# Turned keys stored in the order in which they are loaded, with w_out's counts, the x tiles and the sample softmax reordered

## The reference, cut to what matters

```python
z = rmsnorm(x) @ w_in                      # columns: q (4 heads x 2 x 64), k, v (4 x 128), u_a, v_a
# differential attention, per head
s = einsum(q, k) / 8 + rel_bias            # two maps m = 0, 1
a = softmax(s[0]) - lam * softmax(s[1])
o_b = rmsnorm(a @ v) * (1 - lam_init)
o_a = u_a * (tril(w_spatial) @ layernorm(v_a) + b_spatial)
x = x + rmsnorm(concat(o_b, o_a) @ w_out)
h = causal_conv3(rmsnorm(x) @ w_up); x = x + rmsnorm((silu(h_g) * h_u) @ w_down)
```

## Time and profile before

| | us |
|---|---|
| median of three timed runs | 1334.69 |
| the profiled execution, its own time | 1343.45 |
| its span from first to last instruction | 1341.7 |
| PE busy / DVE / ACT / POOL | 1314.5 / 726.9 / 447.0 / 167.2 |

### The profile page before, as it was taken

How to read it: one execution, slowest core, us unless ns; L and a number is a source line. 1 busy time by engine, 2 the same in 40 slices (tenths; PEclk the granted TensorE clock), 3 DMA queues, 4 the chain that set the end, 5 groups by cost and what they waited for, 6 DMA issues and landing times.

```text
span 1341.7 us, 21889 instructions
## 1 busy us (share of the span) xinstructions
PE 1314.5 (98%) x8364; PEld 1191.9 (89%) x8364; DVE 726.9 (54%) x1185; ACT 447.0 (33%) x764; POOL 167.2 (12%) x323
## 2 busy tenths in 40 slices
PE   7999999999997999999999999999999999999997
PEld 7999999966665888998989899998989898989986
DVE  6446645277776464466454535545464635453556
ACT  6321001057766343441323223231313131323332
POOL 2227000022222211200000000000000000000003
PEclk9999999999998999999999999999999999999999
DMA  8576778369997242321110201020201111020117
GB/s 274 180 253 239 264 221 214 75 170 252 248 261 220 78 141 71 110 79 32 40 54 16 78 16 63 16 78 16 78 16 63 31 63 31 17 77 16 47 48 137
DMA packets 132424, 146.96 MB, mean 110 GB/s; under 512 B 25852, under 2 KB 101285, under 8 KB 132357
## 3 DMA queue, kind: packets, MB, share of 16 engines
q1 hardware_dynamic: 107865, 122.30, 31.3%
q10 hardware_dynamic: 23500, 20.24, 4.7%
q0 software_dynamic: 992, 3.54, 1.6%
HBM read 114.06 MB, written 31.47 MB: 108 GB/s over the span
## 4 chain that ended last, share of the span: by engine, by line
PE 88%; SPq 4%; DMA 4%; issue 2%; DVE 1%; ACT 1%; POOL 0%; POOLq 0%; DVEq 0%; ACTq 0%
PE PS L2515 39%; PE PS L2234 17%; PE PS L2580 16%; PE PS L2459 7%; PE PS L2595 2%; PE PS L2610 2%; SPq L883 2%; DMA x_in<-in_x_prompt_dram 1%; DMA wo_raw<-in_w_out_dram 1%; DMA kt_a<-keys_t 1%; SPq L893 1%; PE PS L2285 1%; SPq L894 1%; PE PS L2325 1%; PE PS L2388 1%
## 5 line engine op out<-in xcount | busy, mean ns | idle before, releaser
L2515 PE MATMUL PS<-act_lo,wu_hi 128*128 128x364 f32 (+1 forms) x1056 | 346.4, 328 | 0.0
L2515 PE MATMUL PS<-act_hi,wu_lo 128*128 128x364 f32 (+1 forms) x1056 | 346.0, 328 | 0.0
L2515 PE MATMUL PS<-act_hi,wu_hi 128*128 128x364 f32 (+1 forms) x1056 | 345.9, 328 | 0.0
L2515 PEld LDWEIGHTS PS<-act_hi,wu_hi 128*128 128x128 f32 x1056 | 198.5, 188 | 0.5
L2515 PEld LDWEIGHTS PS<-act_lo,wu_hi 128*128 128x128 f32 x1056 | 198.2, 188 | 0.4
L2515 PEld LDWEIGHTS PS<-act_hi,wu_lo 128*128 128x128 f32 x1056 | 198.3, 188 | 0.0
L1999 DVE TENSOR_TENSOR y_acc<-y_acc,PS 128x512 f32<-128x512 f32 x162 | 111.2, 687 | 116.0 <-PE PS L2580 116.0
L2580 PE MATMUL PS<-wd_hi,g_hi 128*128 128x512 f32 x324 | 130.1, 401 | 0.0
L2580 PE MATMUL PS<-wd_lo,g_hi 128*128 128x512 f32 x324 | 128.0, 395 | 0.0
L2580 PE MATMUL PS<-wd_hi,g_lo 128*128 128x512 f32 x288 | 114.0, 396 | 0.0
L1362 ACT CAST g_hi<-conv 128x1088 fp32r<-128x1088 f32 x21 | 23.2, 1103 | 245.6 <-PE PS L2580 189.7
(11 more groups left out here) (294 smaller groups left out, 2306.4 us busy)
## 6 DMA issues: line engine op xcount, KB each, us to landing
wu_raw<-in_w_up_dram SPq DMA_DIRECT2D x44, 512.0 KB, 3.8
k_tok<-in_cache_k_dram SPq DMA_DIRECT2D x64, 256.0 KB, 3.7
keys_t<-k_turned ACTq DMA_DIRECT2D x32, 512.0 KB, 4.1
vpage<-in_cache_v_dram SPq DMA_DIRECT2D x64, 256.0 KB, 6.6
wd_raw<-in_w_down_dram SPq DMA_DIRECT2D x22, 512.0 KB, 5.3
w_raw<-in_w_in_dram SPq DMA_DIRECT2D x20, 512.0 KB, 6.4
kt_mid<-keys_t SPq DMA_DIRECT2D x20, 256.0 KB, 8.4
kt_b<-keys_t SPq DMA_DIRECT2D x20, 256.0 KB, 9.6
```

Of the source, the lines that this page charges most:

```text
L2515: mm = nc.tensor.matmul(PS[:, 3 * half + c, 0:kept(c)], a[:, half, k, :], b[:, k, KEPT[c]], start=(j == 0), stop=(j == len(parts) - 1))
```

## The change

1. `keys_t` is laid out by unit, block j, feature d, pair, part i and column c, and no longer by pair, i, d, j, c. A unit's load is then one DMA over 128 partitions in runs of 8 KB in place of four; a pair's store is four DMAs, one for each j, in place of one. The counts of `ktok_stored` and `kt_loaded` follow.
2. `WO_SEM` gives each pair of w_out's rows a count of its own: rows 0 and 1 semaphore 0, rows 4 and 5 semaphore 1, rows 2 and 3, later 6 and 7, semaphore 2; SP waits for rows 2 and 3 before it issues 6 and 7.
3. In the first stage SP issues all x tiles ahead of w_in's second group and the gate's loads. ACT and DVE split that group after the last tile, and PE runs job 8 ahead of the transposes of w_spatial.
4. In the rounds `SMP_LAST` DVE takes the second set's maximum ahead of the sample factors and the mix of the first step, and ACT's second exponent stands ahead of `take_rows`.

```diff
-    keys_t = nc.dram_tensor("keys_t", [4 * NB, 4, 32, 4, 2 * H * 32], F32)
+    keys_t = nc.dram_tensor("keys_t", [2 * NB, 4, 32, 2, 4, 2 * H * 32], F32)
...
+    WO_SEM = [0, 0, 2, 2, 1, 1, 2, 2]
...
-            if s == 4:
-                for p in range(2, 4):
-                    sp.wait_ge(w_lo_ready, p - 1)
-                    load_w(sp, p)
-            if s == 5:
-                sp.dma_start(ws_nat[:], w_spatial[0].rearrange("g t s -> t g s")).then_inc(gate_loaded, 16)
...
+        for p in range(2, 4):
+            sp.wait_ge(w_lo_ready, p - 1)
+            load_w(sp, p)
+        sp.dma_start(ws_nat[:], w_spatial[0].rearrange("g t s -> t g s")).then_inc(gate_loaded, 16)
...
-            for j in range(4):
-                src = bass.AP(keys_t, (2 * u * 4 * 32 * 4 + j) * 256, [[4 * 256, 32], [32 * 4 * 256, 8], [1, 256]])
-                dst = kt[u][32 * j:32 * j + 32].rearrange("a n i p h t -> a (n i) (p h t)")
-                sp.dma_start(dst, src).then_inc(kt_loaded[kt_place(u)], 16)
+            src = keys_t[u].rearrange("j d n i c -> (j d) (n i c)")
+            sp.dma_start(kt[u].rearrange("a n i p h t -> a (n i p h t)"), src).then_inc(kt_loaded[kt_place(u)], 16)
...
-                sp.dma_start(wo_raw[k][:], w_out[0, P * k:P * k + P, :]).then_inc(wo_loaded[k // 4 if k < 6 else 2], 16)
+                sp.dma_start(wo_raw[k][:], w_out[0, P * k:P * k + P, :]).then_inc(wo_loaded[WO_SEM[k]], 16)
...
+        sp.wait_ge(wo_loaded[2], 16 * 2)
         load_w_out(range(6, KD))
...
-            dst = keys_t[n].rearrange("i d j c -> (i d) (j c)")
-            act.dma_start(dst, k_turned[n % 2][:]).then_inc(ktok_stored[n % 2], 16)
+            for j in range(4):
+                dst = keys_t[n // 2, j, :, n % 2].rearrange("d i c -> i d c")
+                act.dma_start(dst, k_turned[n % 2][:, 256 * j:256 * j + 256]).then_inc(ktok_stored[n % 2], 16)
...
-            act.wait_ge(wo_loaded[k // 4 if k < 6 else 2], 16 * (4 if k < 4 else 2))
+            act.wait_ge(wo_loaded[WO_SEM[k]], 16 * (4 if k >= 6 else 2))
...
+            if s in SMP_LAST:
+                smp_exponent(s // RIN - 1, 1)
+                part_exponent(s // RIN - 1)
             if s >= 1:
                 take_rows(before)
...
-                dve.wait_ge(ktok_stored[n % 2], 16 * (n // 2))
+                dve.wait_ge(ktok_stored[n % 2], 64 * (n // 2))
...
+            if s in SMP_LAST:
+                smp_softmax(s // RIN - 1, 1)
             if s in SMP_TURN:
                 smp_factors(SMP_TURN[s])
...
+        pe.wait_ge(xt_lo_ready, 2 * STEPS)
+        project(STEPS - 1)
         pe.wait_ge(gate_loaded, 16 * (4 + NB))
```

More of the change, by code:

```diff
@@ L678, in kt_count @@
     def kt_count(u):
-        return 64 * (sum(kt_place(v) == kt_place(u) for v in range(u)) + 1)
+        return 16 * (sum(kt_place(v) == kt_place(u) for v in range(u)) + 1)
     ring, ring_taken = [], []
@@ L826, in _ @@
                 sp.dma_start(sub_gain[:], subln_gain[0:1, :].to_broadcast([P, DV])).then_inc(setup_loaded, 16)
-            if s == 4:
-                for p in range(2, 4):
-                    sp.wait_ge(w_lo_ready, p - 1)
-                    load_w(sp, p)
-            if s == 5:
-                sp.dma_start(ws_nat[:], w_spatial[0].rearrange("g t s -> t g s")).then_inc(gate_loaded, 16)
[L833 to L839, removed]
+        for p in range(2, 4):
+            sp.wait_ge(w_lo_ready, p - 1)
+            load_w(sp, p)
+        sp.dma_start(ws_nat[:], w_spatial[0].rearrange("g t s -> t g s")).then_inc(gate_loaded, 16)
+        sp.wait_ge(const_ready, 6)
+        for b in range(NB):
+            o = slice(DS * b, DS * (b + 1))
+            sp.dma_start(ws_bd[o, :, o], w_spatial[0, :, 0:DS, 0:DS].rearrange("g t s -> t g s")).then_inc(gate_loaded, 16)
+        sp.dma_start(bs[:], b_spatial[0:1].to_broadcast([P, AG, P])).then_inc(gate_loaded, 16)
+        sp.dma_start(ln_g[:], sgu_ln_gain[0:1, :].to_broadcast([P, AW])).then_inc(gate_loaded, 16)
+        sp.dma_start(ln_b[:], sgu_ln_bias[0:1, :].to_broadcast([P, AW])).then_inc(gate_loaded, 16)
         n_pool = cache_k.shape[1]
@@ L876, in load_keys @@
             if u in (2, 3):
-                sp.wait_ge(kt_loaded[u - 2], 64)
+                sp.wait_ge(kt_loaded[u - 2], 16)
             if u >= 5:
                 sp.wait_ge(sscore_ready, 2 * (u - 3) + 2)
-            for j in range(4):
-                src = bass.AP(keys_t, (2 * u * 4 * 32 * 4 + j) * 256, [[4 * 256, 32], [32 * 4 * 256, 8], [1, 256]])
-                dst = kt[u][32 * j:32 * j + 32].rearrange("a n i p h t -> a (n i) (p h t)")
-                sp.dma_start(dst, src).then_inc(kt_loaded[kt_place(u)], 16)
+            src = keys_t[u].rearrange("j d n i c -> (j d) (n i c)")
+            sp.dma_start(kt[u].rearrange("a n i p h t -> a (n i p h t)"), src).then_inc(kt_loaded[kt_place(u)], 16)
         def load_values(b):
@@ L897, in load_w_out @@
             for k in ks:
-                sp.dma_start(wo_raw[k][:], w_out[0, P * k:P * k + P, :]).then_inc(wo_loaded[k // 4 if k < 6 else 2], 16)
+                sp.dma_start(wo_raw[k][:], w_out[0, P * k:P * k + P, :]).then_inc(wo_loaded[WO_SEM[k]], 16)
         sp.wait_ge(w_lo_ready, 2 * len(GROUPS))
         for i in range(2):
-            sp.wait_ge(ktok_stored[i], 16 * NPAIR // 2)
+            sp.wait_ge(ktok_stored[i], 64 * NPAIR // 2)
         load_keys(0)
@@ L1059, in _ @@
                 take_job(s - 3)
-            if s == 7:
-                act_split_w(act, 1)
             if s == 4:
@@ L1065, in _ @@
         xt_hi(STEPS - 1)
+        act_split_w(act, 1)
+        take_job(STEPS - 3)
         act.wait_ge(ws_turned, 1)
@@ L1070, in _ @@
         nc.scalar.copy(wbT[:], PS[0:NS, 3, 0:AG * NS].rearrange("p (g t) -> p g t", g=AG)).then_inc(ws_taken, 1)
-        for n in range(STEPS - 3, STEPS):
+        for n in range(STEPS - 2, STEPS):
             take_job(n)
@@ L1087, in _ @@
         act.wait_ge(dve_took, last_q_took)
-        act.wait_ge(ktok_stored[0], 16 * NPAIR // 2)
+        act.wait_ge(ktok_stored[0], 64 * NPAIR // 2)
         nc.scalar.activation(sq[:], qT[:, :, 0:NS], ACT.Copy, scale=-1.0).then_inc(sqk_ready, 1)
@@ L1621, in _ @@
                 lam_tables()
-            if s == 8:
-                dve_split_w(dve, 1)
         xt_lo(STEPS - 1)
+        dve_split_w(dve, 1)
         split = 1
@@ L1859, in _ @@
                     if half == 0:
-                        dve.wait_ge(ktok_stored[1], 16 * NPAIR // 2)
+                        dve.wait_ge(ktok_stored[1], 64 * NPAIR // 2)
                     nc.vector.tensor_copy(v_smp[0:NS, vh], v_all[0:NS, c, vh]).then_inc(v_kept, 1)
```

8 lines of the change are left out of this document (removed).

## The result

The changed kernel takes 1400.1 us (median of 4 runs, 1398.03 to 1400.44), the kernel before 1334.68: 1.0475 times as long, 95% interval 1.0452 to 1.0498. That is 65.4 us slower; forecast were 60.6 us (1395, range 1355 to 1450). One thing has to be known for the rest: single executions of the kernel before differ by more than its median tells. They took 1332.4 to 1347.0 us in the 29 runs beside the first experiments, and the profiled one (1343.45) is a long one. The changed kernel's profiled execution took 1398.03, so between the two profiles lie only 54.6 us.

A forecast was written before the change was run, and what follows sets the result against it. TensorE was busy 98% of the span, with DMA engines full only in the first third. Terms 65 + 6 - 8.1 - 1 - 1.3 = +60.6 on 1334.7 gave 1395 us, range 1355 to 1450 (0.76).

The forecast's parts named there:

- Stores on four engines: Projections: each new key store runs on 4 of 16 DMA engines, 185 us per engine, ending projections 65 us later.
- 65 + 6: Projections: 65 us of later end from the slow key stores, plus 6 us for PE's lowered clock.
- Time per pair: Projections: 273 us of work per engine over 32 pairs, 8.5 us a pair; last turn at 311, 91 us late.
- Lead: Projections: PE can run eight jobs ahead of the late turns, two of q and six of v, hiding 26 us.
- Clock: Projections: PE's repeated idling lowers its granted clock and adds 6 us, bounds 0 and 26.
- 88 us: Projections: other loads and key rows on the four engines' queues; 79 us as lower bound because packet times overlap.
- ACT's issues: "nothing": Projections: ACT's store issues grow by 66 us, spread over 273 us in which it computes about 22; cost nothing.
- Key loads: 0: Attention: one load a unit lowers DMA share from full to about 0.8; no price of its own on PE.
- w_out's counts: -8.1: Attention: separate counts remove 5.1 us of PE waits and 3.0 us of clock loss; bounds -5 and -10.
- x tiles -1.3: First stage: x tile 6, issued ahead of the gate loads, saves PE's wait, -1.3 us; bounds -2 and 0.
- third softmax -1: Three rounds: PE's 0.73 us waits for s_prob shrink, part comes back; -1 us, bounds -2.2 and +1.5.
- (a): Rival, key stores: they spread over all 16 engines, or more than about nine; only gains left, 1324 us; chance 0.11.

The follow-up runs named there:

- experiment 2: Changed kernel with a pair's four stores cut by part i (outermost dimension 32) instead of by block j: 1330.4 us, ratio 0.9949.
- experiment 4: Kernel before, old layout, with a pair's store cut into four by block j, DRAM side still merging to 128 rows: 1333.8 us, ratio 1.0003.
- experiment 5: Kernel before, one store a pair, with a padding row behind each part so the outermost dimension is 4: 1394.1 us, ratio 1.0412.
- experiment 11: Kernel before, one store a pair, padded to outermost dimension 8, a unit's keys loaded by eight DMAs of 16 partitions: 1346.9 us, ratio 1.0108.
- experiment 1: Kernel before with only the new keys_t layout, its four stores by block j and its one load: 1408.6 us, ratio 1.0534.
- experiment 7: Kernel before with only the new keys_t layout and its load, stored by part i: 1333.2 us, ratio 0.998.
- experiment 6: Changed kernel with even pairs stored by block j and odd pairs by part i: 1357.2 us.
- experiment 12: Kernel before with the new x tiles and third softmax only; old layout and old w_out counts: 1335.5 us, ratio 0.9998.
- experiment 3: Changed kernel with the old keys_t tensor, one store a pair and four loads a unit: 1331.2 us, ratio 0.9967.
- experiment 9: Changed kernel stored by part i, with x tiles, weights and gate loads in the old order: 1332.3 us, ratio 0.998.

## Why the prediction was right, point by point

**Stores on four engines.** Right, and now shown: experiments 2, 4 and 5 separate the outermost dimension from piece size and issue count, and experiment 11 puts a point between. Alone, the store queue kept 0.27 of the sixteen engines busy with an outermost dimension of 4 and 0.50 with 8. Against experiment 2, which has all the rest, the stores cost 1400.1 - 1330.4 = 69.7 us (75.4 between experiments 1 and 7, without the rest); my terms for them were 65 + 6 = 71. All of it arises in the projections: they end 345.17 - 277.51 = 67.7 us later than in experiment 2's profile, and the spans differ by 67.8. The rule that I quoted from the Trainium skill (DMA: Bandwidth & Descriptors, "Why a DMA increments its semaphore by 16 and not by 1") stands behind rows that agree: these 0.27 and 0.50, where 4 and 8 of 16 are 0.25 and 0.50. That they are the lowest-numbered ones no view here shows.

**How the 71 was made up** was less right; that the sum came out is luck, since three errors cancelled. (1) *Time per pair.* Foreseen 8.5 us (273 / 32), measured 248.1 / 31 = 8.0, so the last turn came at 299.7 and not 311. (2) *Lead.* "Eight jobs ahead, 26 us": the last turn is 80.0 us later and the projections end 65.8 later, so 14 us were made up, not 26. Experiment 5 made up 76.6 - 56.1 = 20 (its last job ends at 332.47 + 3.05). (3) *Clock.* With the same 8364 matmuls PE is busy 1325.8 us in the changed kernel and 1310.8 in experiment 2, so some 15 us of the 67.8 between their spans are slower work and 53 are more idle time; I had 6 and 65. One bound was misread as well: dividing 88 us by the 1.06 that I quoted gives 83 and not 79, which takes a share of 1.11; it moves the low end alone, by some 4 us.

**ACT's issues: "nothing".** This step failed. I counted ACT's time over the whole stage, not where in its stream the issues stand. Two things are in the 786 ns median. The shape: no store on four engines was issued in under 525 ns (experiment 5's median is 526), those by part took 309 at least. And the queue: experiment 6 shows the same issues by part at 751 ns behind stores on four engines, 462 without. The issues were 5.7% of the chain, and the key rows behind them another 2.5%. From 244 us on they held the weight split and PE for 17.9 us. The fourfold count isn't what did it: with one issue a pair experiment 5 waits 19.9 us in the same place, and there the key rows' issues are at 1217 ns. I took this hold to be where the lead went, since the eight banks don't help jobs whose weights aren't split; that isn't shown, as experiment 5 was held as long and still made up 20 us.

**Key loads: 0.** Right at the lowest (experiment 7), the share of 0.77 to 0.76 as forecast (0.8), and the wait for kt_mid is gone. What I didn't see is that they, too, remove the late row of w_out.

**w_out's counts: -8.1.** This step failed. The 7.58 and 2.79 us were real, but they belonged to the profiled execution, which stood 8.8 us above the median; I took them from the median as well, and so counted a wait that the median execution doesn't have. Experiment 12 adds that a late key load isn't the counts' doing. Measured: -0.1 (new layout), -4.3 between the medians of experiments 12 and 3, between the lowest -0.2. Between the two profiles my sum did hold: -9.1 foreseen for counts and softmax, -11.2 measured.

**x tiles -1.3 and third softmax -1.** Measured -1.9 and -1.9 at the median; both within their bounds or at them.

**The sum.** Stores 69.7 and the other parts -3.4 (1330.4 - 1333.8) make 66.3 against a measured 65.4. Forecast were +71 and -10.4. The forecast was 5 us low because of the counts, and would have been further off had turn, lead and clock not made up for each other. Of the rivals, (a) is what experiment 2 is (1330.4 where I had 1324): the loss hangs on one line of the store. Its threshold of "about nine engines" was too high, since eight, in 4 KB pieces, leave the end of the projections where it was.

## What to carry to other kernels

A DMA whose sides both look wide can still run on few engines: read the outermost dimension that is left after merging on both sides, and order the loops so that a long one is outermost; here one changed cut of the same stores was worth 70 us. A stage's mean DMA share falls when that happens, so multiply a queue's share by 16 over the engines that carry it before calling it slack. And before a wait in a profile is priced as a gain on the median, compare the profiled execution with the median: if it is longer by as much, the wait may be that difference.

## What the runs showed of the hardware that I had not expected

- What an issue on ACT takes depends on the DMA's shape and on what stands in the queue ahead of it: 309 ns at least by part, 525 with an outermost dimension of 4, 587 with 8 (experiment 11); and at the median 462 for stores by part among themselves (experiment 2), 751 behind stores on four engines (experiment 6). Other stores on that queue are drawn in: the key rows' issue went from 660 to 751 ns at the median in the changed kernel and to 1217 in experiment 5.
- One code had waits of 0, 1.18 and 4.94 us for the same x tile in three profiles. The new order of loads takes the spread of 12 runs from 3.8 to 0.4 us (experiments 9 and 2) and the lowest time down by only 0.8; with the old key loads and counts it is 12.6 us (experiment 12) at the same lowest time (1330.3).
- Splitting 1 MB into eight loads of 16 partitions gave 235 GB/s at a share of 1.05 in the attention (experiment 11), where four of 32 gave 244 at 0.99 and one load of 128 rows of 8 KB gave 266 at 0.76 (experiment 2).
